# All four weight sums of a block-product pair formed on VectorE, in a two-stream macaron trunk layer

## The chip, the cores and the metric

The kernel runs on one core of a Trainium2 chip. The metric is device time in microseconds (us) of one execution, the median of several runs. One further execution is recorded by the hardware profiler; all rows below come from it.

## The reference, cut to what matters

One layer is applied to 512 prompt frames and 32 sample frames of width 1024 (544 columns, called T in the kernel). It has two SwiGLU feed-forward parts with 2816 hidden channels (22 tiles of 128), and a recurrent mixer between them:

```
def swiglu(x, wg, wu, wd):
    return (jax.nn.silu(x @ wg) * (x @ wu)) @ wd

def trunk_layer(x, ...):
    x = x + 0.5 * swiglu(rms_norm(x, g_ffn1), w_ffn1_gate, w_ffn1_up, w_ffn1_down)
    ...                                             # mixer: projections, mLSTM, retention, w_out
    x = x + 0.5 * swiglu(rms_norm(x, g_ffn2), w_ffn2_gate, w_ffn2_up, w_ffn2_down)
```

All inputs are float32. The change touches only how parts of `x @ wg` and `x @ wu` are prepared.

## The kernel before, in words

**Number format.** Each weight tile is split in two by two engines: ScalarE copies it to a rounded tile `w_hi` (fp32r), VectorE subtracts that from the source and writes the rest, `w_lo`. Activations are split in the same way. A product is then three matmul passes (hi*hi, hi*lo, lo*hi).

**Stages of one feed-forward part** (function `ffn` on every engine; n is 0 for the first part, 1 for the second). First `plain` computes 4 hidden tiles of gate and up, in 8 units of 48 matmuls. Then 18 *pairs* follow, in two groups (`PAIRS`: pairs 0 to 7, and 8 to 17), each group followed by `down`, the product with the down weights. A pair p is a 1024 x 256 slice of the gate weights (p even, called e = 0) or of the up weights (p odd, e = 1). It is multiplied as a 2 x 2 block matrix in seven block products (`BLOCKS = 7`, o = 0 to 6) in place of eight. TensorE's `pair` (line 704) runs the seven one after the other, each 12 matmuls of 272 columns, waits for `block_lo` ahead of each, for the split activations (`x_op_ready`) in pair 0, and for ScalarE's copies of finished products (`product_copied`) ahead of block 2, 4 and 6, because a PSUM bank is used again there.

**The weight operands.** The seven products need the four quarters of the slice, and sums of them. Line by line, `source(e, o)` is the SBUF tile of operand o: for even pairs in `w_src`, for odd ones in `w_raw`. SyncE's `load_pair` (line 487) loads five 256 KB blocks per pair, into o = 0, 1, 3, 4 and 5. Then four sums are made:

- operand 1: the loaded quarter (0,1) plus quarter (0,0). GpSimd's `add_blocks` (line 2014) does it with a transfer that reads quarter (0,0) from DRAM a second time and adds it into `source(e, 1)` (line 2020).
- operand 4: quarter (0,1) plus quarter (1,1), in the same way (line 2022).
- operand 2: `sum_t2` (line 1443), VectorE, `source(e, 1) + source(e, 5)` (line 1450).
- operand 6: `sum_t4` (line 1452), VectorE, `source(e, 2) + source(e, 3)` into the tile of operand 2 (line 1457), after operand 2 has been split.

**Order of the work.** Each engine's queue is written out by hand. While TensorE multiplies pair p, ScalarE and VectorE split the operands of pair p + 1. ScalarE's `pair` (line 1135) does for each o: `copy_product` (line 1090, only for o = 0, 1, 2, 4), then `block_to_hi` of the next pair (line 1059, the copy itself is line 1073), and here and there a SiLU. VectorE's `pair` (line 1585) does for each o: at o = 0 `sum_t2` of the next pair, at o = 3 `sum_t4` of the next pair, some additions that make gate and up out of the products, and `block_to_lo` (line 1459, the subtraction is line 1462). Pair 0 has no pair before it: its operands are split during the last three units of `plain` (ScalarE line 1153, VectorE line 1621, which calls `sum_t2(n, 0)` in unit 5 and `sum_t4(n, 0)` in unit 6). During pair 0 itself both engines run `first_pair` (ScalarE line 1115, VectorE line 1563), which besides the operands of pair 1 splits the last four activation operands (`x_to_hi` line 1082, `x_to_lo` line 1472, with the subtraction in line 1480 or 1477). The part that matters there, on VectorE and on ScalarE:

```
x_to_lo(n, 4); sum_t2(n, 1); x_to_lo(n, 5); x_to_lo(n, 6); ...; block_to_lo(n, 1, 2); sum_t4(n, 1)   # VectorE
block_to_hi(n, 1, 2); copy_product(n, 0, 4); block_to_hi(n, 1, 3); block_to_hi(n, 1, 4); ...         # ScalarE
```

Pair 8, the first of the second group, is prepared in the last four units of the first `down` (lines 1183 and 1680 to 1687).

Of the kernel before, what the change touches and what calls it, by code (L numbers as in the profile page):

```python
# [7 lines left out]
ALU = mybir.AluOpType  # L8
# [4 lines left out]
P = 128  # L13
# [31 lines left out]
def hybrid_trunk_step(nc, x_prompt, x_sample, state_mlstm_C, state_mlstm_n, state_mlstm_m, state_ret_R,  # L45
# [65 lines left out]
    NP = 18  # L111
    KH = DT // 2
# [6 lines left out]
    def pair_index(n, p):  # L119
        return NP * n + p  # L120

    def pair_tile(p):

        return STD + 2 * (p // 2)

    def units_before(n, c):

        return U_STD[n] + 2 * STD if c == 0 else U_DOWN[n][0] + 2 * DT

    with ExitStack() as ctx:  # L130
# [8 lines left out]
        def sem(name):  # L139
            return ctx.enter_context(nc.semaphore(name))  # L140
# [168 lines left out]
        def block_of(buf, n, o):  # L309

            q = (2 * (U_DOWN[n][0] % 4) + o) % 8
            return buf[:, q // 2, KH * (q % 2):KH * (q % 2) + KH, :]

        def source(e, o):

            o = 2 if o == BLOCKS - 1 else o
            return w_raw[:, o // 2, KH * (o % 2):KH * (o % 2) + KH, :] if e else w_src[:, o, :, :]
# [102 lines left out]
        block_loaded = [[sem(f"block_loaded{e}_{o}") if o in (0, 1, 3, 4, 5) else None for o in range(BLOCKS)] for e in range(2)]  # L420
        block_summed = [[sem(f"block_summed{e}_{o}") if o in (1, 4) else None for o in range(BLOCKS)] for e in range(2)]
# [29 lines left out]
        def w_rows(w):  # L451
            return w[0].rearrange("(k p) n -> p k n", p=P)
# [543 lines left out]
        def _(act):  # L996
# [48 lines left out]
            def ffn(n, norm):  # L1045
                plain(n, norm)
                for c in range(2):
                    if c == 0:
                        first_pair(n)
                    else:  # L1050
                        block_to_hi(n, PAIRS[1][0], BLOCKS - 1)
                    for p in PAIRS[c][1:] if c == 0 else PAIRS[c]:
                        pair(n, c, p)
                    Q = pair_index(n, PAIRS[c][-1]) // 2
                    pair_h_to_hi(c, PAIRS[c][-1], Q, 1)
                    pair_h_to_hi(c, PAIRS[c][-1], Q, 0)
                    down(n, c)

            def block_to_hi(n, p, o):

                e, P_ = p % 2, pair_index(n, p)
                c = int(p >= PAIRS[1][0])
                if o in (2, 6):
                    act.wait_ge(pair_summed, 2 * P_ + (1 if o == 2 else 2))
                elif o in (1, 4):
                    act.wait_ge(block_summed[e][o], 16 * (P_ // 2 + 1))
                else:
                    act.wait_ge(block_loaded[e][o], 16 * (P_ // 2 + 1))
                if p == PAIRS[c][0]:
                    act.wait_ge(unit_done, units_before(n, c) - 3 + o // 2)  # L1070
                else:
                    act.wait_ge(product_done, BLOCKS * (P_ - 1) + o + 1)
                nc.scalar.activation(block_of(w_hi, n, o), source(e, o), ACT.Copy).then_inc(block_hi, 1)  # L1073

            def next_hi(n, c, p, o):

                if p + 1 in PAIRS[c]:
                    block_to_hi(n, p + 1, o)
                elif o in (3, 5):
                    split_hi(0, U_DOWN[n][c] + (o - 3) // 2, 0)  # L1080
# [176 lines left out]
            a = half * DT // 2  # L1257
# [132 lines left out]
        def _(dve):  # L1390
# [52 lines left out]
            def sum_t2(n, p):  # L1443

                e, P_ = p % 2, pair_index(n, p)
                dve.wait_ge(block_summed[e][1], 16 * (P_ // 2 + 1))
                dve.wait_ge(block_loaded[e][5], 16 * (P_ // 2 + 1))
                if P_ > 1:
                    dve.wait_ge(block_lo, BLOCKS * (P_ - 1))
                nc.vector.tensor_tensor(source(e, 2), source(e, 1), source(e, 5), ALU.add).then_inc(pair_summed, 1)  # L1450

            def sum_t4(n, p):

                e, P_ = p % 2, pair_index(n, p)
                dve.wait_ge(block_lo, BLOCKS * P_ + 3)
                dve.wait_ge(block_loaded[e][3], 16 * (P_ // 2 + 1))
                nc.vector.tensor_tensor(source(e, 6), source(e, 2), source(e, 3), ALU.add).then_inc(pair_summed, 1)
# [127 lines left out]
            def pair(n, c, p):  # L1585
                e, Q = p % 2, pair_index(n, p) // 2
                more = p + 1 in PAIRS[c]
                for o in range(BLOCKS):
# [5 lines left out]
                    if o == 3 and more:  # L1594
                        sum_t4(n, p + 1)
# [152 lines left out]
            for c, half in X_BY_DVE:  # L1748
                dve.wait_ge(x_moved, X_PIECES.index((c, half)) + 1)
                if c < NC:  # L1750
                    tiles = dense[c % 2][:, half, :].rearrange("p (k d) -> p k d", d=P)
                    a = half * DT // 2
# [239 lines left out]
        def _(pool):  # L1992
# [11 lines left out]
            def add_square(i, j, norm, step, reset=False):  # L2004
                if reset:

                    pool.wait_ge(norm_sums, norm)
                    link(nc.gpsimd.memset(sq_sum[:, :], 0.0))
                pool.wait_ge(sq_ready, DT * (norm - 1) + j + 1 + step * i)
                if not reset:  # L2010
                    pool.wait_ge(sq_added, DT * (norm - 1) + j + step * i)
                nc.gpsimd.tensor_tensor(sq_sum[:, :], sq_sum[:, :], sq[:, :], ALU.add).then_inc(sq_added, 1)

            def add_blocks(n, p, w):

                e, P_ = p % 2, pair_index(n, p)
                a = pair_tile(p) * P
                quarter = lambda k, m: w_rows(w)[:, KH * k:KH * (k + 1), a + m * P:a + (m + 1) * P]
                pool.wait_ge(block_loaded[e][1], 16 * (P_ // 2 + 1))
                nc.gpsimd.dma_start(source(e, 1), quarter(0, 0), accum_op=ALU.add).then_inc(block_summed[e][1], 16)  # L2020
                pool.wait_ge(block_loaded[e][4], 16 * (P_ // 2 + 1))
                nc.gpsimd.dma_start(source(e, 4), quarter(1, 1), accum_op=ALU.add).then_inc(block_summed[e][4], 16)

            def ffn(n, norm, w_gate, w_up):
                for p in range(NP):
                    add_blocks(n, p, (w_gate, w_up)[p % 2])
                pool.wait_ge(pair_h_lo, NP * (n + 1))
                for j in range(DT - 1):
                    add_square(0, j, norm + 1, 0, reset=j == 0)
                    if n == 0 and j == DT - 2:  # L2030

                        pool.wait_ge(unit_done, U_GATE - 3)
                        nc.gpsimd.memset(w_hi[:, U_GATE % 4, :, :].bitcast(F32), 0.0).then_inc(gate_slots_zeroed, 1)

            link(nc.gpsimd.memset(sq_sum[:, :], 0.0))
            def spread_sums(n, c):
                r = P if c < NC else TS
                pool.wait_ge(x_summed, n + 1)
                nc.gpsimd.tensor_scalar(sq_sum[0:r, CH[c]], ident[0:r, 0:r], x_sums[0:r, c:c + 1], None, ALU.mult)\
                    .then_inc(x_sums_spread, 1)  # L2040

            for n, c in enumerate(X_ORDER[:-1]):
                spread_sums(n, c)
            spread_sums(NC, NC - 1)
            ffn(0, 0, w_ffn1_gate, w_ffn1_up)


            pool.wait_ge(unit_done, U_GATE)
# [77 lines left out]
            for j in range(DT):  # L2126
                add_square(0, j, 2, 0, reset=j == 0)

            ffn(1, 2, w_ffn2_gate, w_ffn2_up)


# [27 lines left out]
```

## Time and profile before

| | |
|---|---|
| median of 3 runs | 1067.53 us (1067.3 to 1067.54) |
| the profiled execution's own time | 1067.17 us |
| its span in the trace | 1065.4 us |
| TensorE matmul busy | 1055.7 us, 99% |
| VectorE busy | 686.5 us, 64% |
| ScalarE busy | 467.0 us, 44% |
| GpSimd busy | 191.6 us, 18% |
| software (GpSimd) DMA queue | 19.72 MB, 14.6% of the 16 engines' span |
| granted TensorE clock | mean 0.998 of full speed |

The profile divides the span into engine time, and its views show who waited for whom. TensorE is busy from end to end, so the time moves only where TensorE starts to wait, or stops waiting. In the timeline, a row's start is when the instruction began. VectorE's and ScalarE's instructions overlap their neighbour's end by about 0.1 us, so the cost of one more instruction in a full queue is the distance between two starts, not its duration.

### The profile page before, as it was taken

What the parts mean: (1) busy time and instruction counts of PE and PEld (TensorE: products, weight loads), DVE (VectorE), ACT (ScalarE), POOL (GpSimd) and SP (SyncE); (2) the same over time, 40 slices, a digit from 0 to 9 for tenths busy, and PEclk for the clock granted to TensorE, in tenths of its full rate; (3) what the DMA queues carried; (4) which work ended last, traced back from release to release, by engine and by line L of the source; (5) the groups of instructions that cost most, each with busy time, mean ns of one, the idle gap of its engine ahead of it and who ended that gap; (6) DMA issues with size and microseconds to landing.
All of it is one profiled execution on the core that took longest, in us unless ns stands there. A gap on an engine that the chain in (4) does not pass through costs nothing.

```text
span 1065.4 us, 20474 instructions
## 1 busy us (share of the span) xinstructions
PE 1055.7 (99%) x8424; PEld 1052.1 (99%) x8424; DVE 686.5 (64%) x1162; ACT 467.0 (44%) x818; POOL 191.6 (18%) x168
## 2 busy tenths in 40 slices
PE   8999999999999999999999999999999999999997
PEld 8999999999999999999999999999999999999997
DVE  6998752357866676655655556698875235777544
ACT  7466641256663335433222224436664124666323
POOL 1122100012201211210332222212210002220111
PEclk9999999999999999999999999999999999999999
DMA  7489572388843377445464224547958338882422
GB/s 224 91 186 201 113 187 82 101 161 175 173 87 92 69 131 143 70 70 79 71 80 74 68 77 61 140 94 171 201 109 188 91 92 159 180 175 58 117 75 84
DMA packets 245349, 127.84 MB, mean 120 GB/s; under 512 B 9180, under 2 KB 243716, under 8 KB 245128
## 3 DMA queue, kind: packets, MB, share of 16 engines
q1 hardware_dynamic: 206888, 106.79, 41.3%
q0 software_dynamic: 38288, 19.72, 14.6%
q8 instruction: 67, 1.10, 0.4%
q14 instruction: 26, 0.21, 0.1%
q10 hardware_dynamic: 80, 0.02, 0.0%
HBM read 123.22 MB, written 3.29 MB: 119 GB/s over the span
## 4 chain that ended last, share of the span: by engine, by line
PE 97%; DVE 1%; DMA 1%; SPq 0%; ACT 0%; issue 0%; ACTq 0%
PE dense L589 52%; PE dense L737 30%; PE core_banks L737 5%; PE core_banks L589 3%; PE core_banks L885 1%; PE core_banks L900 1%; PE core_banks L903 1%; PE core_banks L875 1%; DMA x_tok<-in_x_prompt 1%; PE dense L659 1%; PE dense L787 1%; PE core_banks L871 0%; PE core_banks L869 0%; PE core_banks L912 0%; DVE xg_lo L1410 0%; PE core_banks L774 0%
## 5 line engine op out<-in xcount | busy, mean ns | idle before, releaser
L1405 DVE TENSOR_TENSOR w_lo<-w_raw,w_hi 128x1024 fp32r<-128x1024 f32 (+2 forms) x119 | 132.8, 1133 | 54.7 <-ACT w_hi L1025 54.5
L1025 ACT ACTIVATE w_hi<-w_raw 128x1024 fp32r<-128x1024 f32 (+2 forms) x119 | 106.3, 906 | 89.0 <-PE dense L589 81.4
L589 PE MATMUL dense<-h_hi,w_hi 128*128 128x272 f32 x684 | 142.4, 290 | 0.0
L589 PE MATMUL dense<-xg_hi,w_hi 128*128 128x272 f32 x672 | 142.1, 293 | 0.0
L589 PE MATMUL dense<-h_lo,w_hi 128*128 128x272 f32 x684 | 141.1, 287 | 0.0
L589 PE MATMUL dense<-h_hi,w_lo 128*128 128x272 f32 x684 | 140.9, 287 | 0.0
L589 PE MATMUL dense<-xg_lo,w_hi 128*128 128x272 f32 x672 | 138.9, 288 | 0.0
L589 PE MATMUL dense<-xg_hi,w_lo 128*128 128x272 f32 x672 | 138.8, 288 | 0.0
L737 PE MATMUL dense<-x_op_hi,w_lo 128*128 128x272 f32 x432 | 124.6, 289 | 0.0
L737 PE MATMUL dense<-x_op_hi,w_hi 128*128 128x272 f32 x432 | 124.5, 288 | 0.0
L737 PE MATMUL dense<-x_late_hi,w_lo 128*128 128x272 f32 x432 | 124.5, 288 | 0.0
L737 PE MATMUL dense<-x_late_hi,w_hi 128*128 128x272 f32 x432 | 124.3, 288 | 0.0
L737 PE MATMUL dense<-x_late_lo,w_hi 128*128 128x272 f32 x432 | 124.2, 287 | 0.0
L737 PE MATMUL dense<-x_op_lo,w_hi 128*128 128x272 f32 x432 | 124.0, 287 | 0.0
L1462 DVE TENSOR_TENSOR w_lo<-w_src,w_hi 128x512 fp32r<-128x512 f32 x126 | 85.8, 689 | 49.8 <-ACT w_hi L1073 49.7
L1712 DVE SCALAR_TENSOR_TENSOR xT<-dense,xT 128x544 f32<-128x544 f32 x38 | 27.5, 724 | 135.3 <-PE dense L589 135.3
L589 PEld LDWEIGHTS dense<-h_lo,w_hi 128*128 128x128 f32 x684 | 107.9, 188 | 0.0
L589 PEld LDWEIGHTS dense<-h_hi,w_lo 128*128 128x128 f32 x684 | 106.8, 188 | 0.0
L589 PEld LDWEIGHTS dense<-h_hi,w_hi 128*128 128x128 f32 x684 | 106.7, 188 | 0.1
L589 PEld LDWEIGHTS dense<-xg_lo,w_hi 128*128 128x128 f32 x672 | 105.8, 188 | 0.0
L589 PEld LDWEIGHTS dense<-xg_hi,w_lo 128*128 128x128 f32 x672 | 105.1, 188 | 0.0
L589 PEld LDWEIGHTS dense<-xg_hi,w_hi 128*128 128x128 f32 x672 | 104.7, 188 | 0.2
(332 smaller groups left out, 2216.8 us busy)
## 6 DMA issues: line engine op xcount, KB each, us to landing
w_src<-in_w_ffn_gate SPq DMA_DIRECT2D x90, 256.0 KB, 4.6
w_raw<-in_w_ffn_up SPq DMA_DIRECT2D x90, 256.0 KB, 3.7
w_raw<-in_w_in SPq DMA_DIRECT2D x32, 512.0 KB, 8.9
w_raw<-in_w_ffn_down SPq DMA_DIRECT2D x32, 384.0 KB, 4.0
w_raw<-in_w_ffn_down SPq DMA_DIRECT2D x32, 320.0 KB, 3.5
w_src<-in_w_ffn_gate POOLq DMA_DIRECT2D x36, 256.0 KB, 5.3
w_raw<-in_w_ffn_up POOLq DMA_DIRECT2D x36, 256.0 KB, 5.6
w_raw<-in_w_ffn_up SPq DMA_DIRECT2D x8, 512.0 KB, 4.7
```

Source lines behind the costliest of these rows:

```text
L589: last = nc.tensor.matmul(out[:, half, 0:TH], w[:, s % 4, k, :], x(kt)[:, half * TH:(half + 1) * TH], start=start and n == 0 and m == 0, s ...
L659: last = nc.tensor.matmul(bank_of(1)[:, half, 0:TH], w[:, 1, k, :], part(k)[:, half * TH:(half + 1) * TH], start=w is w_hi and k == 0 and ...
L737: last = nc.tensor.matmul(banks[BANK[o]], w[:, k, :], x[:, k, :], start=o in OPENS and k == 0 and m == 0, stop=k == KH - 1 and m == 2, ski ...
L787: last = nc.tensor.matmul(bank_of(t)[:, part, 0:cols.stop - cols.start], w[:, (s + u) % 4, kt - a, :], x[:, kt, cols], start=kt == 0 and m ...
L875: nc.tensor.matmul(X[:, 3, CH[c]], p(h, 1, CH[c]), p(h, 0, CH[c]), start=True, stop=True)
L885: last = nc.tensor.matmul(X[:, b, o * V1:(o + 1) * V1], k_tail[:, c, :], v_tok[:, c, :], start=True, stop=True)
L900: last = nc.tensor.matmul(out, score_tail[:, block], v_tok[:, c, :], start=True, stop=c == 0)
L903: last = nc.tensor.matmul(out, sum_ident[:, block], state, start=False, stop=True)
L1025: nc.scalar.activation(w_hi[:, s % 4, 0:k_tiles(s), :], raw, ACT.Copy).then_inc(w_hi_ready, 1)
L1405: nc.vector.tensor_tensor(w_lo[:, s % 4, 0:nk, :], w_raw[:, s % RAW, 0:nk, :], w_hi[:, s % 4, 0:nk, :].bitcast(F32), ALU.subtract).then_in ...
L1462: nc.vector.tensor_tensor(block_of(w_lo, n, o), source(p % 2, o), block_of(w_hi, n, o).bitcast(F32), ALU.subtract)\
L1712: nc.vector.scalar_tensor_tensor(x, halves(tile), factor, x, ALU.mult, ALU.add).then_inc(evicted, 1)
```

## The change

The transfers that add into operands 1 and 4 are gone, and with them `add_blocks`; GpSimd's queue has nothing in the pair stage. VectorE makes both sums: operand 1 at the head of `sum_t2`, with a wait for its own result behind it, and operand 4 at the head of `sum_t4`. The semaphores `block_summed` are now raised by VectorE, by 1.

```
@@ scalar, block_to_hi @@
                 elif o in (1, 4):
-                    act.wait_ge(block_summed[e][o], 16 * (P_ // 2 + 1))
+                    act.wait_ge(block_summed[e][o], P_ // 2 + 1)
@@ vector @@
             def sum_t2(n, p):
                 e, P_ = p % 2, pair_index(n, p)
-                dve.wait_ge(block_summed[e][1], 16 * (P_ // 2 + 1))
+                dve.wait_ge(block_loaded[e][0], 16 * (P_ // 2 + 1))
+                dve.wait_ge(block_loaded[e][1], 16 * (P_ // 2 + 1))
+                nc.vector.tensor_tensor(source(e, 1), source(e, 1), source(e, 0), ALU.add).then_inc(block_summed[e][1], 1)
+                dve.wait_ge(block_summed[e][1], P_ // 2 + 1)
                 dve.wait_ge(block_loaded[e][5], 16 * (P_ // 2 + 1))
...
             def sum_t4(n, p):
                 e, P_ = p % 2, pair_index(n, p)
+                dve.wait_ge(block_loaded[e][4], 16 * (P_ // 2 + 1))
+                nc.vector.tensor_tensor(source(e, 4), source(e, 4), source(e, 5), ALU.add).then_inc(block_summed[e][4], 1)
                 dve.wait_ge(block_lo, BLOCKS * P_ + 3)
...
@@ gpsimd @@
-            def add_blocks(n, p, w):
-
-                e, P_ = p % 2, pair_index(n, p)
-                a = pair_tile(p) * P
-                quarter = lambda k, m: w_rows(w)[:, KH * k:KH * (k + 1), a + m * P:a + (m + 1) * P]
-                pool.wait_ge(block_loaded[e][1], 16 * (P_ // 2 + 1))
-                nc.gpsimd.dma_start(source(e, 1), quarter(0, 0), accum_op=ALU.add).then_inc(block_summed[e][1], 16)
-                pool.wait_ge(block_loaded[e][4], 16 * (P_ // 2 + 1))
-                nc.gpsimd.dma_start(source(e, 4), quarter(1, 1), accum_op=ALU.add).then_inc(block_summed[e][4], 16)
-
-            def ffn(n, norm, w_gate, w_up):
-                for p in range(NP):
-                    add_blocks(n, p, (w_gate, w_up)[p % 2])
+            def ffn(n, norm):
                 pool.wait_ge(pair_h_lo, NP * (n + 1))
...
-            ffn(0, 0, w_ffn1_gate, w_ffn1_up)
+            ffn(0, 0)
...
-            ffn(1, 2, w_ffn2_gate, w_ffn2_up)
+            ffn(1, 2)
```

## Rows read from the trace of the kernel before

**Rows 1.** The page's first part: busy time, share, instructions.

```profile
PE 1055.7 (99%) x8424; PEld 1052.1 (99%) x8424; DVE 686.5 (64%) x1162; ACT 467.0 (44%) x818; POOL 191.6 (18%) x168
```

**Rows 2.** Waits: of TensorE the longest; ScalarE for the down weights.

```profile
PE core_banks L824 <- POOL eps L2002: 1.9, 1, 1.9
...
ACT w_hi L1025 <- DMA w_raw<-in_w_ffn_down: 3.0, 2, 2.7
```

**Rows 3.** Windows (pairs 1, 3, 4): length, busy PE, PEld, DVE, ACT, POOL, clock, DMA.

```profile
73.00:83.54 10.54, 10.54 (x87) 10.54 (x86) 10.47 (x21) 6.84 (x14) 2.56 (x2) 1.00 0.86 211
...
94.07:104.60 10.53, 10.53 (x86) 10.53 (x86) 7.88 (x15) 6.74 (x14) 2.56 (x2) 1.00 0.88 178
104.60:115.13 10.53, 10.53 (x86) 10.53 (x86) 8.66 (x16) 6.67 (x13) 1.67 (x2) 1.00 0.86 175
```

**Rows 4.** VectorE's groups: one of the sums that it makes now.

```profile
L1450 DVE TENSOR_TENSOR w_src<-w_src 128x512 f32<-128x512 f32 x18 | 12.3, 684 | 0.0
```

**Rows 5.** VectorE's timeline, steady stage (start, duration, ..., idle before).

```profile
99.57 0.69 DVE L1462 TENSOR_TENSOR w_lo<-w_src,w_hi 128x512 fp32r<-128x512 f32 x1 [0.81 <-ACT w_hi L1073]
```

**Rows 6.** VectorE's timeline, first part, unit 6 of plain to pair 0.

```profile
56.72 0.69 DVE L1462 TENSOR_TENSOR w_lo<-w_src,w_hi 128x512 fp32r<-128x512 f32 x1 [1.05 <-ACT w_hi L1073]
57.45 0.69 DVE L1457 TENSOR_TENSOR w_src<-w_src 128x512 f32<-128x512 f32 x1
...
63.28 0.73 DVE L1671 TENSOR_TENSOR h_f<-dense,gate_r 128x544 f32<-128x544 f32 x1
...
66.54 1.29 DVE L1480 TENSOR_TENSOR x_late_lo<-x_sum,x_late_hi 128x1088 fp32r<-128x1088 f32 x1 [0.31 <-ACT x_late_hi L1087]
67.75 0.68 DVE L1450 TENSOR_TENSOR w_raw<-w_raw 128x512 f32<-128x512 f32 x1
68.35 1.28 DVE L1480 TENSOR_TENSOR x_late_lo<-x_sum,x_late_hi 128x1088 fp32r<-128x1088 f32 x1
...
72.95 0.68 DVE L1462 TENSOR_TENSOR w_lo<-w_raw,w_hi 128x512 fp32r<-128x512 f32 x1
73.66 0.69 DVE L1457 TENSOR_TENSOR w_raw<-w_raw 128x512 f32<-128x512 f32 x1
```

**Rows 7.** TensorE's timeline: first matmul of block 4 and 5, pair 0.

```profile
68.34 0.28 PE L737 MATMUL dense<-x_late_hi,w_hi 128*128 128x272 f32 x1
...
69.85 0.29 PE L737 MATMUL dense<-x_late_hi,w_hi 128*128 128x272 f32 x1
```

**Rows 8.** ScalarE's timeline, first part, pair 0 into pair 1.

```profile
64.04 0.66 ACT L1175 ACTIVATE h_hi<-h_f 128x544 fp32r<-128x544 f32 x1 [0.34 <-DVE h_f L1671]
...
70.81 1.68 ACT L1073 ACTIVATE w_hi<-w_raw 128x512 fp32r<-128x512 f32 x3
73.06 0.43 ACT L1104 ACTIVATE sq<-sq 128x272 f32<-128x272 f32 x1 [0.58 <-DVE sq L1508]
74.39 0.63 ACT L1073 ACTIVATE w_hi<-w_raw 128x512 fp32r<-128x512 f32 x1 [0.89 <-DVE w_raw L1457]
74.92 0.38 ACT L1094 ACTIVATE kept<-dense 128x272 f32<-128x272 f32 x1
```

**Rows 9.** TensorE's timeline where it had waited for VectorE.

```profile
16.51 0.52 PE L646 MATMUL dense<-xg_lo,w_hi 128*128 128x272 f32 x2 [0.15 <-DVE xg_lo L1410]
```

**Rows 10.** VectorE's timeline, second part, unit 7 and pair 0.

```profile
730.56 0.72 DVE L1671 TENSOR_TENSOR h_f<-dense,gate_r 128x544 f32<-128x544 f32 x1 [1.85 <-PE dense L589]
...
735.33 0.69 DVE L1450 TENSOR_TENSOR w_raw<-w_raw 128x512 f32<-128x512 f32 x1
735.93 1.29 DVE L1480 TENSOR_TENSOR x_late_lo<-x_sum,x_late_hi 128x1088 fp32r<-128x1088 f32 x1
...
740.52 0.69 DVE L1462 TENSOR_TENSOR w_lo<-w_raw,w_hi 128x512 fp32r<-128x512 f32 x1
```

**Rows 11.** TensorE's timeline, second part: first matmul of block 4.

```profile
736.38 0.28 PE L737 MATMUL dense<-x_late_hi,w_hi 128*128 128x272 f32 x1
```

**Rows 12.** GpSimd's timeline: one of its 72 adding transfers.

```profile
66.08 1.27 POOL L2022 DMA_DIRECT2D w_src<-in_w_ffn_gate  x1 [3.28 <-DMA w_src<-in_w_ffn_gate]
```

## The prediction

> **What bounds the kernel now.** The page comes first: TensorE's matmuls fill 99% of the span [rows 1]. The list of waits asks what stops TensorE: its longest wait, 1.9 us, is at the start and has nothing to do with the change, and neither VectorE's weight sums nor the adding transfers stand there [rows 2]. The windows show one pair each: 10.53 us, all of it TensorE at full granted clock [rows 3]. So there is nothing on the path for the change to take away. What matters is how much cover each added VectorE instruction has. On average there is plenty (DVE 64% [rows 1]), but the windows show a stage with another limit: in pair 1 VectorE is busy 10.47 of 10.54 us, against 8.66 and 7.88 us in pairs 4 and 3 [rows 3]. So I read the timelines of the first two pairs instruction by instruction.
>
> **What goes.** GpSimd issues 72 adding transfers fewer, 1.27 us each on its own queue [rows 12], and 256 KB less is read each time. No engine that TensorE waits for is behind them: worth 0.
>
> **What is added.** Each of 36 pairs gets two VectorE additions of a 128x512 tile, the size of the sums already there, 0.68 us long [rows 4]. In a full queue such an instruction costs the distance to the next start: 67.75 to 68.35, 0.60 us [rows 6]. Behind an instruction whose result is awaited the distance is 0.73 or 0.71 us instead (56.72 to 57.45, 72.95 to 73.66) [rows 6].
> - `sum_t2`: one addition and a wait for itself: +0.71 us.
> - `sum_t4`: the old line 1457 waits for the subtraction just ahead of it. The new addition needs no such wait and fills that time: 0.60 + 0.60 + 0.60 in place of 0.73 + 0.60, so +0.48 us (between 0.47 and 0.49).
>
> That is +1.19 us per pair on VectorE, 43 us in all.
>
> The Trainium skill bears on the self-wait (VectorE: DVE Perf Modes, section "The DRAIN you can't avoid"): a semaphore between chained instructions costs nothing extra. By that the additions would cost 0.60 and 0.60, or 1.20 per pair; the rows show 0.11 to 0.13 us for the wait, so the trace disagrees. By the page the sum below would be about 0.2 us smaller, because only `sum_t2`'s share is then 0.60.
>
> **Steady stage: 0.** In pair 4, 8.66 + 1.19 = 9.85 us is under 10.53. The idle time is in the right place: VectorE waits up to 0.81 us for a single `w_hi` [rows 5], which itself waits for TensorE, so `sum_t2`'s delay is made up within the first three operands of the same pair. The operands split there are needed a whole pair later. If that cover were gone, each microsecond too much would count in every pair (rival 3). Pair 8 is prepared during `down`, where VectorE idles: 0.
>
> **Entry of the first part.** The additions for pair 0 lie in `plain`, units 5 and 6, in a queue that is full from there on. The one idle stretch, 1.05 us at 56.72 [rows 6], absorbs nothing: ScalarE's copy comes behind an eviction that VectorE itself makes late. So `h_f`, the last eviction, moves from 63.28 by 1.19 us. ScalarE's `h_hi` at 64.04 follows it at once [rows 8], and its chain ends with the operand that VectorE's line 1480 awaits at 66.54 [rows 6].
> 1. Block 4 of pair 0 needs that subtraction. It starts at 66.54 + 1.19 = 67.73, lasts 1.29 and releases TensorE 0.03 us later: 69.05. TensorE is due at 68.34 [rows 7]. Late by 0.71 us.
> 2. `sum_t2` for pair 1 stands directly behind. The next subtraction moves from 68.35 to 68.35 + 1.19 + 0.71 = 70.25 and releases block 5 at 71.57, due 69.85 [rows 7]. Late by 1.72 us in all (not in addition). Block 6 and the first operands of pair 1 then have 0.3 us and more in hand.
> 3. The new dependence: ScalarE's copy of operand 4 of pair 1 now waits for VectorE's addition in `sum_t4`. Before, it was done in the batch at 70.81 [rows 8]. The addition comes behind the subtraction at 72.95, now 72.95 + 1.90 = 74.85: start 75.45, done 76.14. What is queued behind on ScalarE: copies 4, 5 and 6 of pair 1 (0.53 us from start to start, 74.39 to 74.92 [rows 8]), a SiLU (0.43 long [rows 8], 0.35 in a full queue, an estimate from the overlap), and then `copy_product` of pair 1's block 0, which TensorE awaits ahead of block 2. It starts at 76.17 + 3 x 0.53 + 0.35 = 78.11 and ends at 78.51. With 1.505 us per block (69.85 - 68.34) block 2 was due at 68.34 + 5 x 1.505 = 75.87, and starts at 78.54. Late by 2.67 us in all.
>
> From there VectorE catches up: the next such point, block 4 of pair 1, clears by 0.1 us by the same working. A restart costs TensorE a little: two matmuls take 0.52 us where 0.41 is usual, after a wait for VectorE [rows 9]. Only the last counts, +0.11; the others are swallowed by the next wait. **First part: +2.8 us.**
>
> **Entry of the second part.** Here `h_f` waits 1.85 us for TensorE [rows 10], more than the 1.19, so the first delay vanishes. `sum_t2` adds 0.71: the subtraction at 735.93 ends at 735.93 + 0.71 + 1.29 + 0.03 = 737.96, against block 5's 736.38 + 1.505 = 737.89 [rows 10, 11]: 0.07. Point 3 returns: 740.52 + 0.71 + 0.60 + 0.69 + 0.03 = 742.55, plus 1.94 of queued ScalarE work, plus 0.40 and 0.03: 744.92, due 736.38 + 7.53 = 743.91. Late by 1.0 us, with the restart **+1.1 us**.
>
> **Sum.** 1067.17 + 2.8 + 1.1 = 1071.1 us for the profiled execution; the median shown is 0.36 us above that execution: **1071.4 us**, +0.36%. A difference under 0.2% (2.1 us) is about what a measurement of this kernel cannot tell from no change. Bounds of the terms: the first part between 1.8 (points 1 and 2 alone, with a restart) and 3.7 (0.1 us more for each of VectorE's new waits, and the 0.1 us at block 4 lost). The second between 0.1 and 1.8.
>
> **Rivals.**
> 1. **The copy is not in the way** (0.20). If point 3 has over 1 us more cover than I count, only points 1 and 2 remain: 1.8 + 0.1 us, 1069.4 us, within the 0.2%. For it: it is a chain through three engines, summed from single distances. Against: the order is fixed in the code, and ScalarE already waits 0.89 us for line 1457 before (74.39 [rows 8]).
> 2. **Faster** (0.03). The adding transfers slow someone. The place would be a load: ScalarE waits 3.0 us in all for down weights [rows 2]. If freed bandwidth took that off TensorE's path, and the entries had full cover, 1064.5 us. It decides only if TensorE waits there, and it does not [rows 2]. A second way is VectorE's own speed beside GpSimd: the subtraction at 66.54 takes 1.29 us while GpSimd's instruction runs from 66.08 to 67.35 [rows 12], and its neighbour at 68.35, without one, takes 1.28 [rows 6], so nothing is to be had. The Trainium skill (SBUF — State Buffer, "Who interferes with whom") has a VectorE instruction with two SBUF inputs contend with a GpSimd instruction that reads SBUF; by this pair of rows these transfers are none.
> 3. **The steady stage tips over** (0.09). If VectorE ends each pair later than it began, TensorE waits in every one. The price: pair 4's 9.85 us plus the two forced waits for `w_hi` that no reordering fills, about 0.8 us each [rows 5], would be 11.4 against 10.53 us, 0.9 us in each of the some 14 even pairs, +13 us: 1080 us or more. It decides once the waits cannot be filled by the additions; against it, `sum_t2` stands directly ahead of them.
> 4. **The change does not do what it says** (under 0.01): both additions are plainly on VectorE.
>
> **How the numbers follow.** The forecast has 0.67, rival 1 0.20, rival 2 0.03, rival 3 0.09. Slower by over 0.2%: 0.67 + 0.09, less a little for a low sum: 0.75. Within: 0.22. Faster: 0.03. Range: from rival 1's low side, 1068.8, to 1067.53 + 3.7 + 1.8 and a little of rival 3: 1074.
>
> **What would show it.** TensorE's waits should name VectorE's line 1480 (about 1.8 us, twice or three times) and ScalarE's line 1094 (about 0.8 and 1.0 us), all between pair 0 and pair 1 of each part, and ScalarE should wait some 3.5 us for the new addition there. Windows from pair 3 on stay at 10.53 us with VectorE near 9.8. I am wrong if line 1094 is missing from the list, if later pairs stretch, or if TensorE's waits come to under 2 us.

## Result, and the profile after

The changed kernel takes **1071.81 us** (median of 6 runs, 1071.22 to 1072.26). The kernel before, timed beside it, takes 1067.44 us (six runs, one of them at 1070.05, the others 1067.30 to 1067.54). The ratio is 1.0040, 95% interval 1.0029 to 1.0050: slower by 4.4 us, as forecast (1071.4 us, range 1068.8 to 1074.0). The profiled execution of the changed kernel took 1072.1 us.

The page's first part answers to [rows 1], and its last line on the DMA queues shows what the kernel reads:

```profile
PE 1057.3 (99%) x8424; PEld 1052.4 (98%) x8424; DVE 724.6 (68%) x1234; ACT 465.8 (44%) x818; POOL 99.0 (9%) x96
...
HBM read 104.34 MB, written 3.29 MB: 101 GB/s over the span
```

VectorE has 72 instructions more (1234 against 1162) and 38.1 us more busy time. GpSimd has 72 fewer and is idle in the pair stage. The kernel before read 123.22 MB, so the 72 second reads of 256 KB are gone. TensorE is still 99% busy, so 4 us must be sought in its waits. The list of waits, first TensorE's longest, then the ones of ScalarE on VectorE's new and moved additions (engine, line, what it waited for: us in total, times, longest), answers to [rows 2]:

```profile
PE dense L737 <- ACT kept L1094: 2.4, 3, 1.2
PE core_banks L824 <- POOL eps L2007: 1.9, 1, 1.9
...
PE dense L737 <- DVE x_late_lo L1485: 0.5, 1, 0.5
...
ACT w_hi L1073 <- DVE w_raw L1459: 7.1, 2, 3.6
ACT w_hi L1073 <- DVE w_src L1448: 2.5, 2, 1.2
```

Four waits of line 737, 2.9 us in all, are new: three for ScalarE's copy of a finished product, one for VectorE. The same four stand in TensorE's timeline (start, duration, idle before), which answers to [rows 7, 11]:

```profile
67.29 0.39 PE L737 MATMUL dense<-x_op_hi,w_hi 128*128 128x272 f32 x1 [1.16 <-ACT kept L1094]
...
72.68 0.39 PE L737 MATMUL dense<-x_late_hi,w_hi 128*128 128x272 f32 x1 [0.52 <-DVE x_late_lo L1485]
...
79.58 0.40 PE L737 MATMUL dense<-x_op_hi,w_hi 128*128 128x272 f32 x1 [0.62 <-ACT kept L1094]
...
748.73 0.39 PE L737 MATMUL dense<-x_op_hi,w_hi 128*128 128x272 f32 x1 [0.62 <-ACT kept L1094]
```

In order: block 2 of pair 0, block 5 of pair 0, block 2 of pair 1, and block 2 of pair 1 in the second part. The list has no other wait in the 36 pairs.

These waits sum to 2.9 us and the kernel lost 4.4, because a wait costs more than the idle time that the list counts. The idle time starts at the end of the last matmul, 0.29 us after its start, while the next one usually starts 0.125 us after it: 0.16 us more. Then comes the restart, 0.11 us. So each of the four costs 0.27 us beyond its row, the first one 1.16 + 0.27 = 1.43 us. Two stops are too short for a row of their own: 0.09 us at block 4 of pair 0, and 0.22 us at block 5 of pair 0 in the second part. With them the sum is 3.20 and 1.11 us, the lateness of the two parts in the table below.

The windows of pairs 2, 3 and 4 (columns as in [rows 3]) show why the later pairs don't wait:

```profile
87.37:97.90 10.53, 10.53 (x86) 10.53 (x86) 10.21 (x20) 6.67 (x13) 0.00 (x0) 1.00 0.51 148
97.90:108.43 10.53, 10.53 (x86) 10.53 (x86) 9.06 (x18) 6.72 (x14) 0.00 (x0) 1.00 0.44 127
108.43:118.96 10.53, 10.53 (x86) 10.53 (x86) 9.53 (x18) 6.67 (x13) 0.00 (x0) 1.00 0.44 127
```

A pair still takes 10.53 us at full granted clock, all of it TensorE. VectorE catches up in pair 2 (10.21 us busy) and has 1.5 and 1.0 us to spare in pairs 3 and 4.

Who makes TensorE late is read from the two engines behind it. VectorE's timeline answers to [rows 6, 10]:

```profile
54.31 0.72 DVE L1663 TENSOR_TENSOR gate_r<-gate_s,rstd 128x544 f32<-128x544 f32 x1
55.53 0.72 DVE L1676 TENSOR_TENSOR h_f<-core_banks,gate_r 128x544 f32<-128x544 f32 x1 [0.51 <-issue]
...
58.50 0.69 DVE L1467 TENSOR_TENSOR w_lo<-w_src,w_hi 128x512 fp32r<-128x512 f32 x1 [1.05 <-ACT w_hi L1073]
59.11 0.69 DVE L1459 TENSOR_TENSOR w_src<-w_src 128x512 f32<-128x512 f32 x1
59.71 0.69 DVE L1462 TENSOR_TENSOR w_src<-w_src 128x512 f32<-128x512 f32 x1
...
70.01 0.69 DVE L1448 TENSOR_TENSOR w_raw<-w_raw 128x512 f32<-128x512 f32 x1
70.73 0.69 DVE L1453 TENSOR_TENSOR w_raw<-w_raw 128x512 f32<-128x512 f32 x1
71.34 1.29 DVE L1485 TENSOR_TENSOR x_late_lo<-x_sum,x_late_hi 128x1088 fp32r<-128x1088 f32 x1
...
76.53 0.68 DVE L1459 TENSOR_TENSOR w_raw<-w_raw 128x512 f32<-128x512 f32 x1
...
734.38 0.72 DVE L1676 TENSOR_TENSOR h_f<-dense,gate_r 128x544 f32<-128x544 f32 x1 [0.64 <-PE dense L589]
```

L1448 is the new addition for operand 1, L1459 that for operand 4; L1453 and L1462 are the old sums. ScalarE's timeline answers to [rows 8]:

```profile
66.30 0.66 ACT L1175 ACTIVATE h_hi<-h_f 128x544 fp32r<-128x544 f32 x1 [1.29 <-DVE h_f L1676]
66.86 0.38 ACT L1094 ACTIVATE kept<-dense 128x272 f32<-128x272 f32 x1
...
77.25 1.16 ACT L1073 ACTIVATE w_hi<-w_raw 128x512 fp32r<-128x512 f32 x2 [3.55 <-DVE w_raw L1459]
78.31 0.42 ACT L1104 ACTIVATE sq<-sq 128x272 f32<-128x272 f32 x1
78.63 0.61 ACT L1073 ACTIVATE w_hi<-w_raw 128x512 fp32r<-128x512 f32 x1
79.15 0.37 ACT L1094 ACTIVATE kept<-dense 128x272 f32<-128x272 f32 x1
```

The chain of the largest step can be read down the two fences: VectorE's addition runs from 76.53 to 77.21, ScalarE stands 3.55 us for it, then splits operands 4 and 5, applies a SiLU, splits operand 6, and only then copies the product, 79.15 to 79.52. TensorE starts at 79.58.

**A measure for the runs.** The median says how much, not where. So each trace was laid beside that of before: the start of the first matmul of block 3 of a pair, less the same matmul's start before. From that is taken the offset that the first part already had at its row-sum matmul (22.23 us in the trace before), which has nothing to do with the change: between -0.26 and +0.63 us, and +0.63 in the profiled execution of the changed kernel, which is in line with its lying 0.3 us above its median. What is left is the lateness that the pair stage made:

| kernel | pair 0 | pair 1 | pair 17 | second part adds | median less median before |
|---|---|---|---|---|---|
| the changed kernel | 1.43 | 3.20 | 3.20 | 1.12 | 4.4 |
| entry_by_transfer | 0.00 | 0.01 | 0.31 | 0.01 | 0.4 |
| entry_by_vector | 1.41 | 3.17 | 3.17 | 1.12 | 4.1 |
| op4_of_pair1_early | 1.41 | 2.56 | 3.25 | 1.18 | 4.6 |
| op1_only_on_vector | 0.94 | 1.81 | 2.16 | 0.57 | 2.8 |
| both_additions_early | 1.40 | 2.54 | 2.53 | 0.48 | 3.0 |
| op4_only_on_vector | 0.28 | 1.33 | 1.32 | 0.37 | 1.7 |
| steady_plus_1 | 1.40 | 3.16 | 3.13 | 1.11 | 4.0 |
| steady_plus_3 | 1.43 | 3.19 | 9.44 | 7.87 | 17.6 |
| entry3_by_transfer | 0.00 | 0.00 | -0.02 | 0.01 | 0.2 |
| entry3_by_gpsimd | 4.98 | 5.18 | 5.17 | 0.20 | 6.2 |
| all_by_gpsimd | 4.97 | 5.06 | 5.06 | 0.83 | 5.7 |
| three_additions_early | 1.30 | 2.40 | 2.39 | 0.50 | 2.9 |

For pair 17 plus the second part (and 0.62 us in the mixer, in op1_only_on_vector alone) the sum agrees within 0.2 us with each profiled execution's own difference from the 1067.17 us of before, less its offset. The median of a kernel lies up to 1.1 us from its profiled execution, hence the looser agreement with the last column.

### The profile page after: what moved, and what is told of

It is laid out like the page before. It is cut to its first block, busy times and chain, and to the rows that moved or that the text cites. A ratio compares the mean times of both kernels' runs of the same rounds, so it can differ in the third digit from the quotient of the medians.

```text
span 1070.4 us, 20510 instructions
## 1 busy us (share of the span) xinstructions
PE 1057.3 (99%) x8424; PEld 1052.4 (98%) x8424; DVE 724.6 (68%) x1234; ACT 465.8 (44%) x818; POOL 99.0 (9%) x96
## 4 chain that ended last, share of the span: by engine, by line
PE 90%; DVE 2%; issue 1%; ACT 1%; ACTq 0%; DVEq 0%
PE dense L589 50%; PE dense L737 28%; PE core_banks L737 5%; PE core_banks L589 2%; PE core_banks L885 1%; PE core_banks L900 1%; PE core_banks L903 1%; PE core_banks L875 1%; PE dense L787 1%; DVE w_lo L1467 0%; PE core_banks L912 0%; PE core_banks L871 0%; PE core_banks L869 0%; PE core_banks L774 0%; DVE x_late_lo L1485 0%
```

## Experiments

Against the changed kernel, line numbers shift by up to 15 in kernels with more code; the instruction's names tell which one it is. All edits are made to the changed kernel.

### Is it the entry, and only the entry?

Two opposite kernels: in the first only pairs 0 and 1 of each part are summed by transfers as before, in the second (`p not in (0, 1)`) only they are summed on VectorE. The transfers are those of before, with semaphores of their own.

```
+        def by_transfer(p, o):
+            return p in (0, 1)
...
+                if by_transfer(p, 1):
+                    dve.wait_ge(block_added[e][1], 16 * sums_made(P_, 1))
+                else:
...
+            def add_blocks(n, p, w):
...
```

> The changed kernel, but in pairs 0 and 1 of both parts operands 1 and 4 are made by adding transfers as before; the other 16 pairs of each part have all four sums on VectorE. Entry theory (all of the cost arises where pair 0 and pair 1 are prepared, and the steady stage covers the additions): no TensorE wait of the pair stage is left, 1067.4 us, within 0.3 us of before, VectorE near 9.3 us per 10.53 us pair from pair 3 on. Rival (the cost is spread over the pairs, or comes from the longer program): 1071 to 1072 us, as the change.

Measured: 1067.66 us against 1067.31 us before, ratio 1.0003 (0.9994 to 1.0012). This is the entry theory's time but for 0.3 us, told of below.

> The opposite: in pairs 0 and 1 of both parts all four sums are on VectorE, in all others operands 1 and 4 are made by adding transfers as before. Entry theory: the whole cost of the change, 1071.4 to 1071.8 us, with TensorE waiting for ScalarE's line of the product copies in both parts and for VectorE's activation split in the first. Rival (cost spread over the pairs): 8 of 72 additions, so under 1 us: 1068 us.

Measured: 1071.40 us, ratio 1.0039 (1.0026 to 1.0053), as the entry theory expected. TensorE's waits are those of the changed kernel again:

```profile
PE dense L745 <- ACT kept L1104: 2.4, 3, 1.2
...
PE dense L745 <- DVE x_late_lo L1499: 0.5, 1, 0.5
```

So the additions of two pairs in 18 bring the whole cost, and with them there those of the other sixteen add nothing (3.20 and 1.12 us late in the changed kernel, 3.17 and 1.12 here). Without them one other pair shows a little: the first kernel kept 0.3 us in its first part, from block 4 of pair 1 on. ScalarE's timeline has the cause: the operand split that stands ahead of the product copy which block 4 of pair 1 needs waits for pair 2's sum, which in this kernel is already on VectorE:

```profile
77.97 0.63 ACT L1083 ACTIVATE w_hi<-w_src 128x512 fp32r<-128x512 f32 x1 [1.64 <-DVE w_src L1461]
```

### Pair 2 by transfer too

The same with `p in (0, 1, 2)`: 12 adding transfers are left of 72.

> As entry_by_transfer, but pair 2 too has operands 1 and 4 made by adding transfers; VectorE sums from pair 3 on. In the run with pairs 0 and 1 alone, one wait of 0.3 us was left at block 4 of pair 1 in the first part, put down to ScalarE's copy of operand 1 of pair 2, which waits for VectorE's addition. If that is right, no TensorE wait is left in the pair stage: 1067.3 us, the time before. Rival (the 0.3 us are of another kind): 1067.6 us again.

Measured: 1067.36 us against 1067.21, ratio 1.0001 (0.9992 to 1.0010). TensorE has no wait in the pair stage; the longest of its waits is the one at the start, as before:

```profile
PE core_banks L832 <- POOL eps L2021: 1.9, 1, 1.9
```

This also settles the forecast's rival 2: 60 of 72 transfers are gone with full cover at the entry, and no gain shows (the interval leaves room for 0.9 us).

### Each of the two additions alone

`by_transfer` returns `o == 4` (operand 1 on VectorE) or `o == 1` (operand 4 on VectorE), for all pairs.

> Only operand 1 is summed on VectorE, in all pairs; operand 4 is made by adding transfers as before. By the prediction's working with the sum_t4 term taken out: 0.71 us at h_f, block 5 of pair 0 late by 1.24 us in the first part and by 0.07 in the second, no late product copy, restarts 0.11 each: +1.5 us, 1069.0 us (1069.4 with the issue gap). If the copy's wait came from operand 1 too: above 1070.5. If the terms were simply proportional to the number of additions: +2.2 us, 1069.6.

Measured: 1070.15 us, ratio 1.0029 (1.0018 to 1.0039), above what was expected. Pair 0 and 1 are as reckoned (0.94 and 1.81), but two things were not: 0.35 us at block 4 of pair 1 in each part, and a wait in the mixer between the parts, of another place altogether, that stands in this kernel alone:

```profile
PE dense L597 <- DVE rows L1816: 0.5, 1, 0.5
```

What brings that one up was not tried. It was read in the profiled execution, which is 0.5 us longer than the median; whether every execution has it is not known.

> Only operand 4 is summed on VectorE, in all pairs; operand 1 is made by adding transfers as before. By the prediction's working with the sum_t2 term taken out: 0.48 us at h_f, block 5 of pair 0 late by 0.3 us, the product copy late by 1.25 us in the first part and 0.30 in the second, restarts 0.11 each: +1.8 us, 1069.1 us. The issue gap ahead of h_f (0.4 us) has stood only where operand 1 of pair 0 is added on VectorE, so it is not expected. If the order of the queues did not matter and only the number of additions did, as much as with operand 1 alone: 1070.1 us.

Measured: 1069.01 us, ratio 1.0016 (1.0007 to 1.0025), as expected: 1.33 us in the first part where 1.36 was worked out, 0.37 in the second where it was 0.41. Operand 4 delays `h_f` by 0.48 us, less 0.30 of slack, plus 0.11 for the restart: 0.29, measured 0.28. For operand 1 the same sum is 0.71 + 0.41 (the gap of the last section) - 0.30 + 0.11 = 0.93, measured 0.94. So the cost of an addition is known per addition.

### Is it the order on VectorE or the amount of work?

The third point of the forecast says that operand 4's addition for pair 1 stands too late. It can be moved ahead into an earlier place of `first_pair`, with no work removed (`add_4` is that addition with its wait, split off from `sum_t4`; `add_1` below is the same for operand 1 in `sum_t2`):

```
+            def add_4(n, p):
...
+                if p != 1:
+                    add_4(n, p)
...
                 x_to_lo(n, 6)
+                add_4(n, 1)
```

> The changed kernel with one instruction of each part moved: the addition of operand 4 of pair 1 stands behind the last activation split of pair 0 instead of behind the split of operand 2 of pair 1; same instructions, same count. My point 3 (ScalarE's copy of operand 4 waits for that addition and holds up the product copy): ScalarE's wait of 3.55 us for it shrinks to under 1 us, TensorE's late start of block 2 in pair 1 falls from 3.1 to about 2.1 us in the first part and from 1.0 to about 0.4 in the second; the sum is +2.5 us over before, and 0.4 more if the issue gap of 0.4 us seen in the changed kernel's first part is there again: 1070.0 to 1070.4 us. Rival (the copy is held up by something else, or the addition costs the same wherever it stands): 1071.8 us.

Measured: 1071.87 us, ratio 1.0042 (1.0030 to 1.0055). **The total missed, the mechanism held.** ScalarE waits 0.77 us for the addition instead of 3.55. By block 3 of pair 1 TensorE is 2.56 us late instead of 3.20, and 0.48 in the second part instead of 1.12. But by block 3 of pair 2 the 0.7 us are back, in both parts. TensorE's timeline, then ScalarE's:

```profile
82.06 0.40 PE L737 MATMUL dense<-x_late_hi,w_hi 128*128 128x272 f32 x1 [0.43 <-ACT kept L1094]
...
751.28 0.39 PE L737 MATMUL dense<-x_late_hi,w_hi 128*128 128x272 f32 x1 [0.44 <-ACT kept L1094]
```

```profile
81.09 0.63 ACT L1073 ACTIVATE w_hi<-w_src 128x512 fp32r<-128x512 f32 x1 [1.99 <-DVE w_src L1448]
81.63 0.38 ACT L1094 ACTIVATE kept<-dense 128x272 f32<-128x272 f32 x1
```

These are block 4 of pair 1. TensorE, no longer held up at block 2, comes to it sooner, and there the same pattern stands once more: a product copy behind an operand split, behind VectorE's addition, this time of operand 1 for pair 2 (L1448). In the changed kernel this place was hidden by the wait ahead of it. So the second edit moves both:

```
                 x_to_lo(n, 6)
+                add_4(n, 1)
...
                 block_to_lo(n, 1, 3)
+                add_1(n, 2)
```

> The changed kernel with two instructions of each part moved: the addition of operand 4 of pair 1 as in the run before, and also the addition of operand 1 of pair 2, from the head of its sum_t2 to behind the split of operand 3 of pair 1. Same instructions, same count. Theory: moving the first addition alone removed the wait at block 2 of pair 1 and let a wait at block 4 of the same pair take its place (0.7 us in each part), because ScalarE's copy of operand 1 of pair 2 waits for VectorE and stands ahead of the next product copy. With both moved neither is left: pair 2 is late by 2.5 to 2.6 us in the first part and by 0.5 in the second, +3.0 us, 1070.4 us. Rival (VectorE is simply short of time there, so any order ends with the same lateness): 1071.8 us.

Measured: 1070.25 us against 1067.30, ratio 1.0027 (1.0017 to 1.0037), as expected: 2.53 and 0.48 us late, the new wait gone. 1.4 us of the 4.4 come back by order alone, each kernel against the kernel before timed beside it (1.3 us by the lateness in the table), with VectorE doing the same work.

> As both_additions_early, with the addition of operand 1 of pair 0 moved too, from the head of its sum_t2 in unit 5 to unit 4 of plain, in VectorE's queue some 4 us sooner. It asks about the issue gap of 0.4 us ahead of h_f in unit 5, which stood in each kernel where that addition was on VectorE. If the gap is tied to the addition and its wait standing close before: it goes, and pair 2 of the first part is late by 2.0 us, 1069.7 us. If it is tied to the position in VectorE's program: it stays, 2.4 us late (the wait of 0.11 us saved), 1070.1 us.

The third addition moved is operand 1 for pair 0, ahead of its place in `sum_t2`, in unit 4 of `plain`. Measured: 1070.07 us against 1067.21, ratio 1.0027 (1.0016 to 1.0038). The addition no longer needs a wait for itself, and the lateness at pair 0 falls by that: 1.40 to 1.30. The gap of 0.5 us ahead of `h_f`, told of in the last section, stayed, so of the two cases above it is the second.

### How much does the steady stage bear?

The addition of line 1453 is repeated k times (k is written out as 1 or 3), each time with a wait for itself, in every pair but 0, 1, 2, 8 and 9, so only work is added and nothing is computed differently:

```
+                if p not in (0, 1, 2, 8, 9):
+                    for _ in range(k):
+                        link_again(nc.vector.tensor_tensor(source(e, 2), source(e, 1), source(e, 5), ALU.add))
```

> The changed kernel with one more VectorE addition (a repeat of operand 2's sum, with a wait for itself, 0.71 us) in each of the 26 pairs that have three or more pairs behind the start of their part (pairs 3 to 7 and 10 to 17), to measure the cover of the steady stage. VectorE is busy 9.2 to 9.4 us there; with 0.7 more it is at 10.0 of 10.53. Entry theory with cover as counted: no change against the changed kernel, 1071.8 us. Rival (the stage is close to tipping, the forced waits cannot be filled): 26 times some 0.3 us or more, 1080 us.

Measured: 1071.27 us, ratio 1.0037 (1.0023 to 1.0050): the time of entry_by_vector. TensorE is 3.13 us late at pair 17, against 3.20 in the changed kernel: a third addition per pair is free as well in these 26 pairs.

> The same with three more additions of 0.71 us: VectorE would need 11.4 of 10.53 us, so it must become the bound. 26 pairs times 0.9 us: +23 us over the changed kernel, about 1095 us; pairs 3 to 7 stretch to 11.4 us in the windows, VectorE near 100%. Were the cover larger than the busy time says, under 1080 us.

Measured: 1084.89 us, ratio 1.0166 (1.0150 to 1.0181). The stage tips over, but by some 10 us less than I expected: by the lateness it costs 13.1 us beyond the entries (17.3 us against the 4.2 of steady_plus_1). VectorE is full and TensorE waits for a product copy that is held up by VectorE, 20 times, three of them at the entries as in the changed kernel. A window of 10 us from pairs 3 and 4, and the wait:

```profile
104.00:114.00 10.00, 9.91 (x78) 9.51 (x77) 9.93 (x19) 6.29 (x13) 0.00 (x0) 1.00 0.45 131
```

```profile
PE dense L738 <- ACT kept L1095: 6.9, 20, 1.1
```

The lateness is 3.17, 3.77, 4.18, 5.25 and 5.69 us in pairs 3 to 7: a pair adds 0.4 to 0.6 us, one of them 1.1. It then stays at 5.69 up to pair 11. Pairs 8 and 9 have no extra addition, which would let VectorE come to pair 10 with time in hand; that is argued, not measured. So 21 pairs pay (10 in the first part, 11 in the second), some 0.6 us each, where 26 pairs with 0.9 us each were expected. Why one that pays costs less than 0.9 us was not worked out. How two more additions would do was not tried.

### On GpSimd instead of VectorE

`nc.gpsimd.tensor_tensor(source(e, 1), source(e, 1), source(e, 0), ALU.add)` and the like for operand 4, in place of the transfers: for pairs 0, 1 and 2, and then for all.

> The additions of operands 1 and 4 of pairs 0, 1 and 2 done by GpSimd as 128x512 additions in SBUF, no adding transfer anywhere; VectorE sums from pair 3 on. An estimate from GpSimd's 128x544 additions in this kernel (1.4 us alone, up to 2.1 us beside VectorE): 1.3 to 2 us each, and the operands landed long before. If GpSimd and VectorE don't hold each other up: 1067.3 us. If each of GpSimd's additions stops VectorE for its length, some four of them fall into VectorE's full stretch of the first part: 1069 to 1072 us.

> All 72 additions of operands 1 and 4 on GpSimd, VectorE with its old two sums per pair. No mutual hindrance: 1067.3 us, VectorE busy as before (8.66 and 7.88 us per pair). Full mutual exclusion: VectorE's 8.3 us and GpSimd's 2 x 1.3 to 2 us exceed 10.53 us, TensorE waits in every pair, 1075 us or more, and VectorE's instructions show longer durations beside GpSimd's.

Measured: 1073.38 us, ratio 1.0061 (1.0047 to 1.0075), and 1072.94 us, ratio 1.0053 (1.0039 to 1.0067). The first is above both of its cases; the second lies between its two. VectorE has nothing more to do than before, and yet TensorE is 5 us late at pair 0. GpSimd's timeline in the first kernel, then VectorE's:

```profile
37.25 1.91 POOL L2041 TENSOR_TENSOR w_src<-w_src 128x512 f32<-128x512 f32 x1 [17.36 <-DMA w_src<-in_w_ffn_gate]
...
61.45 1.29 POOL L2045 TENSOR_TENSOR w_raw<-w_raw 128x512 f32<-128x512 f32 x1 [2.41 <-DMA w_raw<-in_w_ffn_up]
63.03 2.02 POOL L2041 TENSOR_TENSOR w_src<-w_src 128x512 f32<-128x512 f32 x1 [0.29 <-DMA w_src<-in_w_ffn_gate]
```

```profile
37.24 2.51 DVE L1509 SCALAR_TENSOR_TENSOR x_hat<-xT,gains,rstd 128x544 f32<-128x544 f32 x2
...
40.99 2.31 DVE L1415 TENSOR_TENSOR w_lo<-w_raw,w_hi 128x1024 fp32r<-128x1024 f32 x1
...
60.84 0.72 DVE L1504 TENSOR_TENSOR h_lo<-h_f,h_hi 128x544 fp32r<-128x544 f32 x1
61.47 0.72 DVE L1683 TENSOR_TENSOR sq<-dense,rstd 128x544 f32<-128x544 f32 x1
62.11 1.78 DVE L1496 SCALAR_TENSOR_TENSOR x_op_lo<-x_sum,x_op_hi 128x1088 fp32r<-128x1088 f32 x1
63.81 2.38 DVE L1481 TENSOR_TENSOR w_lo<-w_src,w_hi 128x512 fp32r<-128x512 f32 x2
```

A VectorE instruction with both inputs in SBUF is stretched while a GpSimd addition runs: 1.78 us where 1.28 is usual, 2.38 where two subtractions take 1.29. The one at 61.47, whose input `dense` is in PSUM, keeps its 0.72 beside the same addition. The Trainium skill (SBUF — State Buffer, "Who interferes with whom") has a VectorE instruction with two SBUF inputs contend with a GpSimd instruction that reads SBUF, and one with at most one SBUF input not; these runs agree. Over all pairs the subtraction goes from 689 ns to 826 ns (the group in the page of all_by_gpsimd):

```profile
L1481 DVE TENSOR_TENSOR w_lo<-w_src,w_hi 128x512 fp32r<-128x512 f32 x126 | 102.6, 826 | 25.4 <-ACT w_hi L1083 25.2
```

The stretching is not the whole of the 5 us. It starts early: the two rows at 37.24 and 40.99 took 1.47 and 1.22 us before, and `h_f` of unit 3 is 2.1 us late by them. With the later ones the last `h_f` stands at 66.92, 3.90 us late (63.28 before, and this execution's offset is -0.26). Less 0.30 us of slack that is 3.60, and TensorE's block 2 of pair 0 starts exactly so late. Then another thing begins. TensorE's row there, and the windows around it in the same order of columns as in [rows 3]:

```profile
68.67 0.60 PE L745 MATMUL dense<-x_op_hi,w_hi 128*128 128x272 f32 x1 [3.16 <-ACT kept L1104]
```

```profile
65.40:68.60 3.20, 0.12 (x1) 0.00 (x0) 3.11 (x5) 0.92 (x3) 0.00 (x0) 0.99 0.52 153
68.60:71.90 3.30, 3.23 (x14) 3.23 (x15) 2.66 (x3) 2.93 (x6) 1.53 (x1) 0.50 0.04 11
```

After its idle 3.16 us TensorE has a granted clock of 0.50, its lower level of 1.2 GHz, for 3.3 us, and its matmuls start 0.23 us apart instead of 0.125. The lateness goes from 3.60 us at block 2 to 5.18 within block 3; 0.11 of that is the restart, 1.5 the clock. In all_by_gpsimd it is the same (idle 3.12 us, then a clock of 0.52 in 69.20:72.40; 3.60 to 5.06 us late). In the changed kernel the longest such wait is 1.16 us, and the clock stays at 1.00 through it. So the stretching alone costs the first part 3.7 us, restart included, and the fallen clock the rest.

## Why the prediction was right, and where it was off

**The sum.** Forecast for the first part 2.8 us, measured 3.20; for the second 1.1, measured 1.12. 1067.44 + 3.20 + 1.12 = 1071.76 us, against a median of 1071.81. The forecast's 1071.4 lies 0.4 us below. The excess of the first part is 0.41 us, one gap on VectorE (below); without it, the term was right within 0.01 us.

**The added costs.** `sum_t4` +0.48: in the fence of VectorE 58.50, 59.11, 59.71 in steps of 0.60 where [rows 6] have 0.73. `sum_t2` +0.71: 70.01 to 70.73 is 0.72. (The page's busy time rises by 38.1 us in all, where the working has 43 us of queue time; that difference was not followed up, and nothing in the sum hangs on it.) The wait for its own result costs 0.11 us again, and three_additions_early, where that wait is gone, gains 0.10 at pair 0. The Trainium skill (VectorE: DVE Perf Modes, "The DRAIN you can't avoid") has a chain of eight copies take the same time with a semaphore after each as with one after the last; for these additions the trace of the changed kernel too disagrees, by these 0.11 us.

**Steady stage 0: right.** entry_by_transfer and steady_plus_1 show it, the second with a full addition more. VectorE's busy time in pair 3 rises by 1.18 us (7.88 to 9.06), as worked out; pair 4 reads 9.53, a little under the 9.85 of the sum.

**Point 1: right time, wrong waiter.** I wrote that block 4 of pair 0 would wait 0.71 us for VectorE's subtraction. That subtraction did start where forecast (67.73, plus 0.63 + 0.41 of offset and gap, is 68.77; the trace has it at 68.80), but TensorE was late already. Two blocks earlier it had waited 1.16 us for ScalarE's copy of block 0's product, which stands directly behind `h_hi`. I followed `h_hi` only to the operand split at its end and skipped the `copy_product` in between. ScalarE's row for that copy in the trace before:

```profile
64.61 0.38 ACT L1094 ACTIVATE kept<-dense 128x272 f32<-128x272 f32 x1
```

It ended at 64.99, against a due time of 68.34 - 2 x 1.505 = 65.33 [rows 7]: 0.30 us of slack after the 0.05 to the start. Now it is 1.19 + 0.41 - 0.30 + 0.11 = 1.41 late, measured 1.43 and, in entry_by_vector, 1.41. That the total was not touched is luck: the slip lies on the path, and only because point 2 asks for more than either is it swallowed.

**Point 2: right.** The subtraction ahead of block 5 was forecast for 70.25, with offset and gap 71.29; it starts at 71.34. TensorE's start was forecast for 71.57 + 1.04 = 72.61; measured 72.68. In the second part block 5 is 0.11 us late where 0.07 was worked out.

**Point 3: right.** With the same offset and gap added the steps agree within 0.04 us. Addition forecast at 75.45 + 1.04 = 76.49, measured 76.53. Copy and TensorE's start 78.54 + 1.04 = 79.58, measured 79.58. In the second part 744.92 plus the 3.83 us brought along is 748.75, measured 748.73. It was not the slip of single distances that rival 1 feared; that rival is refuted by op4_of_pair1_early, which takes away this wait and finds it worth 0.64 us in each part, before another takes its place.

**"Block 4 of pair 1 clears by 0.1 us": right, and underrated.** It does clear in the changed kernel: the copy ends at 82.48 and TensorE starts at 82.69. But a margin of 0.1 to 0.2 us behind three waits is the next bottleneck: it took the whole gain of op4_of_pair1_early, 0.35 us in op1_only_on_vector, and 0.31 in entry_by_transfer.

**The second part's cover: right.** `h_f` waits 0.64 us for TensorE where it waited 1.85 [rows 10], so the 1.19 us were taken in full from idle time.

**Rival 3** did not come about: one more addition per pair still costs nothing, and three more tip the stage over.

**The list of late things** named line 1480 (now 1485) two or three times and 1.8 us; it is there once, 0.5 us, and L1094 three times instead of two. That is point 1's slip again.

## What to carry to other kernels

Average cover says nothing at an entry: with VectorE idle for 32% of the span the additions of sixteen pairs in eighteen cost nothing, and those of two, where its queue was full, cost 4.4 us (and pair 2's took 0.3 to 0.7 us where the waits ahead of it were gone). When an instruction is delayed, look at everything queued behind it on every engine down to the last, not only at the operand at the chain's end; here the first waiter was a small copy that stood between two others. And before removing a wait, work out the margin of the next place of the same kind: 0.1 us there means that the wait only moves. Last, look at the granted clock before a whole delay is put down to a wait: with GpSimd adding, 1.5 of 5 us were TensorE's own.

## Not expected of the hardware

**A gap without a cause in the profile.** Ahead of the first part's unit 5 eviction (`h_f`) VectorE idles 0.51 us with "issue" as its releaser: 54.31 to 55.53 is 1.22 us where before, with the same two instructions, it is 0.80. It costs 0.41 us in every later step. In op4_only_on_vector the same two instructions stand without it:

```profile
53.22 0.72 DVE L1677 TENSOR_TENSOR gate_r<-gate_s,rstd 128x544 f32<-128x544 f32 x1
54.03 0.72 DVE L1690 TENSOR_TENSOR h_f<-core_banks,gate_r 128x544 f32<-128x544 f32 x1
```

and with three additions moved it is there, though the addition for pair 0 is a unit earlier:

```profile
54.74 0.72 DVE L1691 TENSOR_TENSOR h_f<-core_banks,gate_r 128x544 f32<-128x544 f32 x1 [0.48 <-issue]
```

It is in all eight kernels with operand 1 of pair 0 on VectorE, and in none of the others nor in any second part. So moving that addition earlier does not remove it, and leaving it out does. What VectorE waits for there stays open.

**GpSimd's own additions.** The shortest takes 1.29 us for 128x512, the longest beside VectorE 2.35 us. With all 72 on GpSimd VectorE is busy 10.46 of 10.50 us in one window of the pair stage (93.30:103.80), and the stage still does not stretch: a stretched instruction fills idle time first. At the entry, where there is none, the same stretching costs the first part 3.7 us, against 3.20 for the additions on VectorE themselves.

**A long wait costs TensorE its clock as well.** The two GpSimd kernels alone have a wait of over 3 us in the pair stage, and they alone ran a stretch of it at half the granted clock. That took 1.5 us and 1.4 us on top of the wait itself. Without it they would be about as slow as the changed kernel, by an estimate from the table: 5.17 + 0.20 - 1.5 = 3.9 and 5.06 + 0.83 - 1.4 = 4.5 us, against 4.3.
